# Short recurrence products placed one or two at a time between the long products of four projection blocks

## The reference

```
proj = h @ w_in                     # q, f, i, g: 1024 columns each
fg = lb + (1 - lb) * sigmoid(f)
q, k, v, logf = silu(q), 1 - fg, i, log(fg)
# per head, in blocks of frames, G = cumsum(logf) within the block:
A = (q_t k_s exp(G_t - G_s)) summed over keys, s <= t
o = A v + (q exp(G)) S
S = exp(G_last) S + (k exp(G_last - G))^T v
o = rms_norm(o, norm_g) * silu(g)
x = x + o @ w_out
```

## Time and profile before

| | |
|---|---|
| median of 3 runs | 4167.85 us (4161.75 to 4168.66) |
| the profiled execution's own time | 4167.03 us |
| its span, first to last instruction | 4165.5 us |
| mean granted TensorE clock | 0.886 |
| busy: TensorE, VectorE, ScalarE | 91%, 52%, 26% |
| the recurrence's steady bodies 2 to 7 (first transpose to first transpose) | 210.24 to 866.37 us, 109.4 us each |

### The profile page before, as it was taken

How to read it: one execution, slowest core, us unless ns; L and a number is a source line. 1 busy time by engine, 2 the same in 40 slices (tenths; PEclk the granted TensorE clock), 3 DMA queues, 4 the chain that set the end, 5 groups by cost and what they waited for, 6 DMA issues and landing times. The chain is left out here.

```text
span 4165.5 us, 55709 instructions
## 1 busy us (share of the span) xinstructions
PE 3777.8 (91%) x19897; PEld 3306.9 (79%) x19897; DVE 2154.1 (52%) x3919; ACT 1086.2 (26%) x1841; POOL 220.5 (5%) x300
## 2 busy tenths in 40 slices
PE   6999999987999999988978689887888799999998
PEld 5988888876999999978964245553558699999997
DVE  5555555546444444455458767775323444444445
ACT  4322222323121111122123234342331312112111
POOL 2000000003000000011000000000000300000000
PEclk8888888878999999999976756666999999999999
DMA  2101011101111111111211100001421111111111
GB/s 87 37 32 37 32 37 37 37 11 33 41 41 46 41 46 36 46 39 54 83 67 41 51 11 11 1 1 59 155 118 41 33 41 41 46 41 46 41 41 58
DMA packets 58108, 187.20 MB, mean 45 GB/s; under 512 B 6984, under 2 KB 23376, under 8 KB 53520
## 3 DMA queue, kind: packets, MB, share of 16 engines
q1 hardware_dynamic: 53216, 165.23, 11.9%
q0 software_dynamic: 4656, 18.65, 1.4%
HBM read 164.28 MB, written 19.57 MB: 44 GB/s over the span
## 5 line engine op out<-in xcount | busy, mean ns | idle before, releaser
L206 PE MATMUL ff1lin<-ff1h_hi,ff1w_hi 128*128 128x384 f32 x1056 | 355.5, 337 | 25.7 <-POOL ff1h_lo L164 15.7
L206 PE MATMUL ff0lin<-ff0h_hi,ff0w_hi 128*128 128x384 f32 x1056 | 356.2, 337 | 22.8 <-POOL ff0h_lo L164 14.2
L207 PE MATMUL ff0lin<-ff0h_lo,ff0w_hi 128*128 128x384 f32 x1056 | 355.4, 337 | 0.0
L208 PE MATMUL ff0lin<-ff0h_hi,ff0w_lo 128*128 128x384 f32 x1056 | 355.1, 336 | 0.0
L208 PE MATMUL ff1lin<-ff1h_hi,ff1w_lo 128*128 128x384 f32 x1056 | 354.8, 336 | 0.0
L207 PE MATMUL ff1lin<-ff1h_lo,ff1w_hi 128*128 128x384 f32 x1056 | 354.8, 336 | 0.0
L206 PE MATMUL hg_lin<-hg_h_hi,hg_w_hi 128*128 128x384 f32 x768 | 269.2, 351 | 17.6 <-POOL hg_h_lo L164 15.7
L207 PE MATMUL hg_lin<-hg_h_lo,hg_w_hi 128*128 128x384 f32 x768 | 263.8, 343 | 0.0
L208 PE MATMUL hg_lin<-hg_h_hi,hg_w_lo 128*128 128x384 f32 x768 | 263.3, 343 | 0.0
L206 PEld LDWEIGHTS ff1lin<-ff1h_hi,ff1w_hi 128*128 128x128 f32 x1056 | 200.0, 189 | 28.1 <-POOL ff1h_lo L164 16.3
L206 PEld LDWEIGHTS ff0lin<-ff0h_hi,ff0w_hi 128*128 128x128 f32 x1056 | 200.3, 190 | 25.3 <-POOL ff0h_lo L164 14.8
(11 more groups left out here) (348 smaller groups left out, 8285.1 us busy)
## 6 DMA issues: line engine op xcount, KB each, us to landing
ff0raw<-in_weights SPq DMA_DIRECT2D x66, 512.0 KB, 3.5
ff1raw<-in_weights SPq DMA_DIRECT2D x66, 512.0 KB, 3.6
hg_raw<-in_weights SPq DMA_DIRECT2D x40, 512.0 KB, 3.5
as_keys<-in_cache_k SPq DMA_DIRECT2D x16, 1024.0 KB, 4.9
as_vals<-in_cache_v SPq DMA_DIRECT2D x8, 2048.0 KB, 9.3
pj_raw<-in_weights SPq DMA_DIRECT2D x18, 512.0 KB, 4.1
se_keys<-in_cache_ki SPq DMA_DIRECT2D x8, 1024.0 KB, 4.9
x<-in_x SPq DMA_DIRECT2D x3, 1536.0 KB, 7.1
```

The lines of the kernel that those rows point to most:

```text
L206: pe.matmul(out, w_hi, x_hi, start=start, stop=False)
L207: pe.matmul(out, w_hi, x_lo, start=False, stop=False)
L208: return pe.matmul(out, w_lo, x_hi, start=False, stop=stop)
```

## The change

Within the recurrence:

- TensorE: the intra-chunk products no longer run in one piece. Two of them follow each unit of the output projection (48 of 64), the rest follow the first nine linear products of the f slab. The 16 updates and the 512-column product follow one by one the last 17 linear products of the f slab; those that overwrite rb[3] come last, and only they wait for the masks. The output products follow, two parts at a time, the linear products 7 to 19 of the v slab. The transposes of v are spread: the first group inside the v slab, the second behind it, the third inside the q slab; the sums of squares move behind q's first group.
- VectorE: the 24 adds come first in the body, with the low part of the f slab after the fifteenth; then masks, v_own, the low part of the v slab, and the chain of states.
- ScalarE: the copies of v are interleaved with its transposes, and the two small exponentials (e_end) come after them.

Where the partner is missing (the output projection in body 1, the projections in body 8), the short products run in one piece.

```diff
+        ATT_PARTS = NC * NS + 1
+        UPDATE_LATE = [c for c in range(NC // 2, NC) if c % 2]
+        UPDATE_ORDER = [c for c in range(NC) if c not in UPDATE_LATE] + UPDATE_LATE
+        UPDATE_PARTS = NC + 1
+        OUTPUT_PARTS = 1 + NC + 1 + DEC_B
+        FIRST_OUTPUT = 7
...
                     hi(h, par0, 2)
-                    hold(act, f_dve, h * 4 + 2, tk)
-                    act.activation(e_end[:, 0:NC], decay[:, CH - 1:T_PROMPT:CH], ACT.Exp)
-                    act.activation(e_end[:, NC:NCH], decay[:, T_PROMPT + DEC_T - 1:T:DEC_T], ACT.Exp)
+                    v_rows(h, base, 0)
...
+                    v_tokens(h, 0)
+                    v_rows(h, base, 1)
+                    v_rows(h, base, 2)
+                    v_tokens(h, 1)
+                    v_tokens(h, 2)
+                    hold(act, f_dve, h * 4 + 2, tk)
+                    act.activation(e_end[:, 0:NC], decay[:, CH - 1:T_PROMPT:CH], ACT.Exp)
...
@@ VectorE, body @@
+                if has(h, 2, 10):
+                    dve.drain()
+                    for nb in range(KB):
+                        for g in range(G):
+                            hold(dve, W.units, units_before(h) + nb * G + g + 1, tk)
+                            xs = x[:, nb, g * GT:(g + 1) * GT]
+                            dve.tensor_tensor(xs, xs, lin[g][:, 0:GT], ALU.add).then_inc(dve_evac, 1)
+                        if nb == KB // 2 and has(h, 0, 8):
+                            lo(h, par0, 0)
                 if has(h, 1, 9):
                     hold(dve, att_done, r + 1, tk)
...
-                if has(h, 0, 8) and body_slabs(h):
-                    lo(h, par0, 0)
...
+                if has(h, 0, 8):
+                    lo(h, par0, 1)
...
@@ TensorE @@
+            def att_part(r, n):
+
+                if n == ATT_PARTS - 1:
+                    pe.matmul(rb[4][:, 0:P], k_mids[:, :], q_mid[:, T_PROMPT:T], start=True, stop=True).then_inc(att_done, 1)
+                    return
+                c, i_ = divmod(n, NS)
+                rows, col, n = c % 2 * CH, c // 2 * CH, SB * (i_ + 1)
+                at = k_at(i_) + c * n
+                pe.matmul(rb[3][rows:rows + n, col + i_ * SB:col + (i_ + 1) * SB], k_mid[:, at:at + n],
+                          q_mid[:, c * CH + i_ * SB:c * CH + (i_ + 1) * SB], start=True, stop=True)
+
+            def update_part(r, n):
+
+                if n == 0:
+                    hold(pe, turned_out, r + 1, tk)
+                if n == UPDATE_PARTS - 1:
+                    hold(pe, v_spread, r + 1, tk)
+                    pe.matmul(rb[4][:, :], k_endT[:, NT - 1, :], v_own[:, 0:4, :].rearrange("p b v -> p (b v)"),
+                              start=True, stop=True).then_inc(ds_done, 1)
+                    return
+                c = UPDATE_ORDER[n]
+                if c == UPDATE_LATE[0]:
+                    hold(pe, att_masked, r + 1, tk)
+                rows = slice(c % 2 * CH, (c % 2 + 1) * CH)
+                i = pe.matmul(ds_at(c), k_endT[rows, c // 2, :], vals[rows, c // 2, :], start=True, stop=True)
+                if n == NC - 1:
+                    i.then_inc(ds_done, 1)
+
+            def output_part(r, n):
+
+                if n == 0:
+                    hold(pe, chained, r * 2 + 1, tk)
+                    pe.matmul(rb[0][:, :], k_endT[:, NT - 1, :], v_own[:, 4:8, :].rearrange("p b v -> p (b v)"),
+                              start=True, stop=True).then_inc(ds_done, 1)
+                elif n <= NC:
+                    c = n - 1
+                    rows = slice(c % 2 * CH, (c % 2 + 1) * CH)
+                    out = rb[1 + c % 2][:, c // 2 * CH:(c // 2 + 1) * CH]
+                    pe.matmul(out, vals[rows, c // 2, :], attT[rows, c // 2 * CH:(c // 2 + 1) * CH], start=True, stop=c == 0)
+                    if c:
+                        pe.matmul(out, states[:, c - 1, :], q_dec[:, c * CH:(c + 1) * CH], start=False, stop=True)
...
+            def turn_v(h, g):
+                hold(pe, v_rows_set, h * 3 + g + 1, tk)
+                for tile in range(3):
+                    i = pe.transpose(lin[g][:, tile * P:(tile + 1) * P], k_endT[:, 3 * g + tile, :], ident[:, :])
+                i.then_inc(v_turned, 1)
+
+            def linear(h, par0, k, kb, g):
+                i = W.product(pe, lin[g][:, 0:GT], pars(par0, h, k), kb * P, h_hi[:, kb, g * GT:(g + 1) * GT],
+                              h_lo[:, kb, g * GT:(g + 1) * GT], kb == 0, kb == KB - 1)
+                if kb == KB - 1:
+                    i.then_inc(W.units, 1)
...
                             W.product(pe, lin[g][:, 0:GT], par0, nb * P, o_hi[:, g * GT:(g + 1) * GT],
                                       o_lo[:, g * GT:(g + 1) * GT], True, True).then_inc(W.units, 1)
+                            if has(h, 1, 9):
+                                if n == 0:
+                                    hold(pe, q_dve, r * 2 + 2, tk)
+                                for part in range(2 * n, 2 * n + 2):
+                                    att_part(r, part)
...
                 if has(h, 0, 8):
                     hold(pe, W.lo_done, slab_no(h, 0) + 1, tk)
+                    for n in range(G * KB):
+                        g, kb = divmod(n, KB)
...
+                        linear(h, par0, 0, kb, g)
+                        if has(h, 2, 9) and n <= 8:
+                            for part in range(48 + 2 * n, min(50 + 2 * n, ATT_PARTS)):
+                                att_part(r, part)
+                        if has(h, 1, 9) and n >= G * KB - UPDATE_PARTS:
+                            update_part(r, n - G * KB + UPDATE_PARTS)
...
                     hold(pe, W.lo_done, slab_no(h, 1) + 1, tk)
+                    for n in range(G * KB):
+                        g, kb = divmod(n, KB)
+                        if kb == 0:
+                            hold(pe, act_evac, h * 12 + g + 1, tk)
+                        linear(h, par0, 1, kb, g)
+                        if has(h, 1, 9) and FIRST_OUTPUT <= n < FIRST_OUTPUT + OUTPUT_PARTS // 2:
+                            for part in range(2 * (n - FIRST_OUTPUT), 2 * (n - FIRST_OUTPUT) + 2):
+                                output_part(r, part)
+                        if n == 2 * KB + 5:
+                            turn_v(h, 0)
+                    turn_v(h, 1)
...
+                    hold(pe, W.lo_done, slab_no(h, 2) + 1, tk)
+                    hold(pe, act_evac, h * 12 + 3 + 1, tk)
+                    for kb in range(KB):
+                        linear(h, par0, 2, kb, 0)
+                        if kb == KB // 2:
+                            turn_v(h, 2)
```

More of the change, by code:

```diff
@@ L498, in body @@
                 r = h - 1
+                if isinstance(h, int) and h == 8:
+                    W.split_lo(dve, 39, 1, 1)
+                if has(h, 2, 10):
[7 more added lines that the diff above has]
+                            lo(h, par0, 0)
                 if has(h, 1, 9):
@@ L539, in body @@
                 if has(h, 0, 8):
-                    lo(h, par0, 1)
                     hold(dve, act_evac, h * 12 + 3, tk)
@@ L650, in body @@
                                       o_lo[:, g * GT:(g + 1) * GT], True, True).then_inc(W.units, 1)
-                if has(h, 1, 9):
-                    hold(pe, turned_out, r + 1, tk)
-                    hold(pe, att_masked, r + 1, tk)
-                    for c in range(NC):
-                        rows = slice(c % 2 * CH, (c % 2 + 1) * CH)
-                        i = pe.matmul(ds_at(c), k_endT[rows, c // 2, :], vals[rows, c // 2, :],
-                                      start=True, stop=True)
-                    i.then_inc(ds_done, 1)
-                    hold(pe, v_spread, r + 1, tk)
-                    pe.matmul(rb[4][:, :], k_endT[:, NT - 1, :], v_own[:, 0:4, :].rearrange("p b v -> p (b v)"),
-                              start=True, stop=True).then_inc(ds_done, 1)
+                            if has(h, 1, 9):
[3 more added lines that the diff above has]
+                                    att_part(r, part)
+                elif has(h, 1, 9):
+                    hold(pe, q_dve, r * 2 + 2, tk)
+                    for part in range(ATT_PARTS):
+                        att_part(r, part)
@@ L672, in body @@
-                if has(h, 1, 9):
-                    hold(pe, chained, r * 2 + 1, tk)
-                    pe.matmul(rb[0][:, :], k_endT[:, NT - 1, :], v_own[:, 4:8, :].rearrange("p b v -> p (b v)"),
-                              start=True, stop=True).then_inc(ds_done, 1)
-                    for c in range(NC):
-                        rows = slice(c % 2 * CH, (c % 2 + 1) * CH)
-                        out = rb[1 + c % 2][:, c // 2 * CH:(c // 2 + 1) * CH]
-                        pe.matmul(out, vals[rows, c // 2, :], attT[rows, c // 2 * CH:(c // 2 + 1) * CH], start=True, stop=c == 0)
-                        if c:
-                            pe.matmul(out, states[:, c - 1, :], q_dec[:, c * CH:(c + 1) * CH], start=False, stop=True)
```

(35 more changed lines are left out.)

71 lines of the change are left out of this document (25 added, 46 removed).

## The result

The changed kernel takes 4263.15 us, median of four runs (4257.83 to 4267.27), beside 4167.4 for the kernel before: a ratio of 1.0231 (95% interval 1.0214 to 1.0247), slower by 95.75 us. The forecast was 4219 with a range up to 4262: the direction was right, the size too small, and the time lies 1.15 us above the range. The profiled execution of after took 4257.83 of its own, 90.8 more than the one before, and this is what is taken apart here.

The account below looks back on a forecast made before the run. TensorE, busy nearly everywhere, was taken to bound the kernel at its granted clock. The profiled 4167 us plus 6 for the weave at high clock plus 46 for falls in four bodies gave 4219, range 4150 to 4262.

Parts of the forecast that it names:

- The weave at the high clock: Bodies 2 to 7 with the clock held high: all savings and switch costs sum to +1.0 us a body.
- -6.3, +8.2, +3.9 and -5.0: Terms per body in us: out-projection -6.3, updates alone between long products +8.2, intra-chunk pairs +3.9, output products -5.0.
- Rival 2: Short weights' loads slip under long products, so groups cost their passes alone: 4085 us; chance 0.17 for hidden or cheaper switches.
- That the clock falls within the woven outputs, as a majority case: V slab: clock falls in some to all woven outputs, late or half way; chance 0.56, 4180 to 4260 us.
- 11.6: V slab: cost in us per body of a clock fall half way through the woven outputs.
- I take 4: Number of the seven bodies whose woven outputs lose the clock, between bounds 0 and 7: +46 us.
- The last body weaves only the out-projection, 24 pairs: -6.3, +2.1, ..., -1: Body 8: out-projection saves 6.3 us, pairs cost 2.1, masks and v_own 3.1 stand before its chain; net -1 us.
- The weave's other two parts are denser, and I take them as high: Woven pairs and updates, 0.52 us long beside 0.45 or 0.64, were taken to run at the high clock.
- The range's upper end: Whole kernel: 4262 us, above the 4260 of a late or half-way fall in all bodies with woven outputs.
- The forecast's own sign of being wrong: A body longer elsewhere, with TensorE waiting for a split or an evacuation by more than 3 us.
- The new VectorE order: VectorE's split in the adds does not matter by itself: beyond the out-projection's 2.73 us wait nothing hangs on it.

Follow-up runs that it names:

- run 5: Changed kernel with slab 39's split behind the adds in body 8 and one chunk's outputs per v-slab step instead of two: 4203.91 us.
- run 1: Changed kernel with one line moved: in body 8 the weight split of slab 39 goes behind VectorE's adds: 4243.91 us.
- run 11: Kernel before with VectorE's new order alone (adds and first split ahead of the masks, slab 39's split behind the adds): 4179.98 us.
- run 4: Changed kernel with nothing woven: intra-chunk products, updates and outputs each in one piece, new VectorE and ScalarE order kept: 4168.69 us.
- runs 3: Changed kernel with the 17 updates of a body in one piece behind the f slab's last step: 4229.12 us.
- run 6: Kernel of run 5 with the updates also in one piece behind the f slab's last step: 4190.54 us.
- run 7: Kernel of run 6 with the updates' piece behind step 14 of the f slab and outputs from step 4 of the v slab: 4117.46 us.
- run 9: Kernel before, unwoven, with only the intra-chunk products reordered: equal sizes of an even and an odd chunk side by side: 4124.45 us.
- run 12: Kernel of run 7, intra-chunk products equal-size paired in one piece, two chunks' outputs every other step, attT products before states products: 4029.51 us.

## Why the forecast was right and where it failed

**The weave at the high clock** was right in its terms: a body of +1.0 us forecast, +1.2 in body 3, out of terms of -6.3, +8.2, +3.9 and -5.0 whose stages came out within 2 us. That the sum agrees to 0.2 is in part luck: the +1.2 is against the mean of before, and against its body 4 (108.28 us), from whose rows the terms were read, body 3 is 2.3 longer. The v slab's stage was 1.8 us above its terms (30.19 against 28.4); the six transposes of v that now stand in it are some 1.0 of that, and the q slab is relieved of them. Rival 2 is out: an update between long products costs 0.62 us and a pair 0.46, not their passes. With rival 2's price the updates of body 3 would have come every 0.77 us; they came every 1.14. In the trace the weight load of an update starts with its own first pass (383.83), while that of a long product behind another starts 0.17 us ahead of it. The rule that the Trainium skill gives in TensorE: Matmul & The Clock Gate, section Step-by-step: what each phase is for, that a weight load is pulled ahead, is thus not borne out where the weight shape changes from 128 rows to 64 and back.

**That the clock falls within the woven outputs, as a majority case**, was right, and run 5 shows that their density matters: behind the same wait, one chunk a step instead of two holds it. Two sizes were off in opposite directions: a fall costs 10.3 us and not 11.6, and it happened in six bodies and not in four. "I take 4" between bounds of 0 and 7 was a middle, not a reading; 15.7 of the missing 38.8 us are this term.

**The step that failed is the one on body 8**: "The last body weaves only the out-projection, 24 pairs: -6.3, +2.1, ..., -1", together with "The weave's other two parts are denser, and I take them as high". The diff showed the split of slab 39 still ahead of the adds in body 8, and I gave this body the same end of the wait as the others. The wait stayed and took the clock with it: body 8 came out at +19.4 and not -1, so that 20.4 of the missing 38.8 us are here, and in run 1 that line alone gives them back (body 8 in 91.9 us and not 111.9). The range's upper end allowed for a fall in all seven bodies with outputs, but not for one in body 8. The forecast's own sign of being wrong, TensorE waiting for a split by more than 3 us, came true here, with 3.08. What I had not asked is what the woven pairs do once the clock is low. They hold a high clock and they do not raise a low one: one mixture, two levels, and the history decides. So a wait of 3 us ahead of a thin stretch costs 20.

**The new VectorE order** "is no case of its own": right (run 11, and run 4 together with the rest).

Of the remaining 2.5 us, 3.7 lie behind the recurrence, in code that the change does not touch; what stands ahead of body 1 became 1.2 shorter. Why was not looked into.

**Open** is what decides, in a given body and run, whether the two-chunk outputs lose the clock. Bodies 3 and 5 of after come to their v slab through stages that agree to 0.01 us (23.50 and 23.49, then 26.59 and 26.60), and one holds where the other falls. It was not settled here. In body 4 TensorE is busy for 41.03 of 42.29 us at a mean clock of 0.68, and all but 0.1 of its idle time is the 1.19 us wait some 7 us ahead of the fall; a longer wait brings the fall forward (runs 3 and 6). No run has two chunks in every step without that wait, so whether the wait is needed for the fall is not shown.

## What to carry to other kernels

Before short products are woven into long ones, ask what the mixture does at either level of the clock: one that holds a high clock may not raise a low one, so any wait ahead of it is multiplied (two waits of 2 us were worth 73 us over seven bodies in run 7). Where a change takes a wait away in a loop, look for the written-out bodies in which it stays. And order short products by weight shape and array half before weaving them at all: a new order in one loop, alone, gained 43 us where the weave lost 96.

## What the runs showed of the hardware

- Neighbouring products with equal weight sizes on opposite column halves run side by side: 35 passes of the intra-chunk products in a microsecond at the high clock (run 9), against 18 when sizes alternate within a half. The same holds for attT products on opposite row halves: four passes take 0.44 us (run 12), as two did in after (0.43); with the states products behind one another, a group of two chunks goes from 1.51 to 1.02 us.
- A stretch in which TensorE is busy throughout can run at 0.50 for as long as it lasts: in body 8 of after the woven out-projection, 32.2 us from 942 to 974, which ran at 1.00 in run 1.
- An idle time of 1.7 us ahead of thin work was followed by a fall 1.9 us after it in body 5 of run 6 (581.76 to 583.7), and in body 7, but not in the other five bodies; one of 1.19 us was not followed by a fall for some 7 us in body 4 of after.
